# Wider low-half pieces on GpSimd, two reorderings in the first MLP and a later place for two modulation chunks, in a two-layer diffusion block on one core

## The reference

```
ml = split(silu(c) @ w_mod[i] + b_mod[i], 6)       # shift, scale, gate for the mixer, the same for the MLP
h  = rms_norm(xl, g) * (1 + ml[1]) + ml[0]
xl = xl + ml[2] * mixer_i(h)                        # layer 0: Fourier + neighbourhood attention, layer 1: differential attention
h  = rms_norm(xl, g') * (1 + ml[4]) + ml[3]
xl = xl + ml[5] * (square(relu(h @ w_mlp_in[i])) @ w_mlp_out[i])
# context tokens the same way in layer 0 with c_ctx; in layer 1 only the latent tokens go on
return rms_norm(xl, final_norm_g)
```

## Time and profile before

| what | value |
|---|---|
| median of 3 runs | 1603.57 us (1601.69 to 1603.67) |
| the profiled execution | 1603.09 us |
| its span in the trace | 1601.3 us |
| TensorE busy | 1573.3 us, 98% |
| GpSimd busy | 910.0 us, 57% |
| VectorE busy | 894.1 us, 56% |
| ScalarE busy | 604.7 us, 38% |
| low halves of units (L744), 776 pieces of 256 columns | 639.4 us, 856 ns each |
| sums of raw blocks into w_sum (L770), 52 pieces | 48.6 us, 965 ns each |

### The profile page before, as it was taken

How to read it: one execution, slowest core, us unless ns; L and a number is a source line. 1 busy time by engine, 2 the same in 40 slices (tenths; PEclk the granted TensorE clock), 3 DMA queues, 4 the chain that set the end, 5 groups by cost and what they waited for, 6 DMA issues and landing times.

```text
span 1601.3 us, 24059 instructions
## 1 busy us (share of the span) xinstructions
PE 1573.3 (98%) x9272; PEld 1408.7 (88%) x9272; DVE 894.1 (56%) x1364; ACT 604.7 (38%) x1009; POOL 910.0 (57%) x1103
## 2 busy tenths in 40 slices
PE   8999999999899999999999999999999999999998
PEld 5889988988899999999998888878889878888887
DVE  4696457347845656647556746049965753232234
ACT  4422456325252342442542511248853412222222
POOL 2443475326677768768762656354415865555562
PEclk9999999999999999999999999999999999999999
DMA  8574212212042232333352223110003332323221
GB/s 350 197 268 153 93 41 100 80 48 85 27 157 81 80 119 82 116 115 123 105 182 82 91 78 96 66 43 1 1 12 130 129 126 93 105 92 101 83 93 53
DMA packets 50348, 163.15 MB, mean 102 GB/s; under 512 B 6336, under 2 KB 8768, under 8 KB 46656
## 3 DMA queue, kind: packets, MB, share of 16 engines
q1 hardware_dynamic: 50240, 161.68, 29.4%
HBM read 158.78 MB, written 2.10 MB: 100 GB/s over the span
## 4 chain that ended last, share of the span: by engine, by line
PE 86%; DVE 6%; POOL 2%; issue 2%; DMA 2%; ACT 1%; SPq 0%; POOLq 0%; DVEq 0%; ACTq 0%
PE ps L2109 24%; PE ps L2110 24%; PE ps L2111 24%; PE ps L2748 3%; PE ps L2710 2%; PE ps L2737 1%; PE ps L2615 1%; POOL w_lo L744 1%; PE ps L2603 1%; PE ps L2643 1%; PE ps L2427 1%; DVE mod_acc L1439 1%; DMA mod_big<-w_mod_dram 1%; DVE h L1562 1%; DMA raw<-units_dram 1%
## 5 line engine op out<-in xcount | busy, mean ns | idle before, releaser
L744 POOL TENSOR_TENSOR w_lo<-raw,w_hi 128x256 fp32r<-128x256 f32 x776 | 639.4, 856 | 492.4 <-ACT w_hi L949 362.0
L2109 PE MATMUL ps<-h,w_hi 128*128 128x512 f32 (+2 forms) x1016 | 358.0, 352 | 7.2 <-POOL w_lo L744 4.6
L2110 PE MATMUL ps<-h,w_lo 128*128 128x512 f32 (+2 forms) x1016 | 355.3, 350 | 0.0
L2111 PE MATMUL ps<-h,w_hi 128*128 128x512 f32 (+2 forms) x1016 | 355.0, 349 | 0.0
L2109 PEld LDWEIGHTS ps<-h,w_hi 128*128 128x128 f32 x1016 | 192.2, 189 | 32.3 <-issue 9.1
L2111 PEld LDWEIGHTS ps<-h,w_hi 128*128 128x128 f32 x1016 | 192.0, 189 | 17.1
L2110 PEld LDWEIGHTS ps<-h,w_lo 128*128 128x128 f32 x1016 | 192.2, 189 | 16.4
L1660 DVE SCALAR_TENSOR_TENSOR xl<-ps,mods,xl 128x384 f32<-128x384 f32 (+2 forms) x144 | 73.0, 539 | 210.8 <-PE ps L2111 209.0
L949 ACT ACTIVATE w_hi<-raw 128x1024 fp32r<-128x1024 f32 x120 | 126.4, 1054 | 113.2 <-PE ps L2111 107.7
L2109 PE MATMUL ps<-hidl,w_hi 128*128 128x384 f32 (+2 forms) x448 | 150.4, 336 | 2.5 <-DVE hidl L1704 1.5
L2110 PE MATMUL ps<-hidh,w_lo 128*128 128x384 f32 (+2 forms) x448 | 149.8, 334 | 0.0
(11 more groups left out here) (301 smaller groups left out, 3181.1 us busy)
## 6 DMA issues: line engine op xcount, KB each, us to landing
raw<-units_dram SPq DMA_DIRECT2D x187, 512.0 KB, 3.4
mod_ring<-w_mod_dram SPq DMA_DIRECT2D x96, 256.0 KB, 3.9
mod_big<-w_mod_dram SPq DMA_DIRECT2D x16, 1024.0 KB, 10.2
mod_late<-w_mod_dram SPq DMA_DIRECT2D x8, 1024.0 KB, 8.1
xl<-x_dram SPq DMA_DIRECT2D x2, 2048.0 KB, 8.3
bias<-bias_dram SPq DMA_DIRECT2D x8, 384.0 KB, 3.7
xc<-ctx_dram SPq DMA_DIRECT2D x2, 1024.0 KB, 10.4
out_dram<-out_t SPq DMA_DIRECT2D x16, 128.0 KB, 1.8
```

Source lines behind the costliest of these rows:

```text
L744: ins = nc.gpsimd.tensor_tensor(w_lo[:, s, sl], src[:, sl], w_hi[:, s, sl].bitcast(F32), op=ALU.subtract)
L2109: mm(out, a[0], b[1], start=start, stop=False, skip_group_check=onto)
L2110: mm(out, a[1], b[0], start=False, stop=False, skip_group_check=onto)
L2111: return mm(out, a[0], b[0], start=False, stop=stop, skip_group_check=onto)
```

## The change

It has three parts.

1. In the first MLP, ScalarE rounds T4 no longer directly after T3 but after the three weight roundings of `next_block(1)`; on VectorE T1's low half and T2's second sum (`join`) change places.
2. Chunks 10 and 11 are made later in the second MLP's first block: of chunk 10 one step after each of hidden tiles 3 to 6 and four, with the split, after tile 7; of chunk 11 two, three and three steps after the additions behind units 8, 9 and 10. TensorE takes the two sums after units 8 and 11, not after 7 and 10, and VectorE extracts each right before the first addition that needs it. The loads of their rows move as well (MOD_LATE).
3. `lows()` and `mlp()` on GpSimd cut units into two pieces of 512 columns. The first three units, `norm()` and the first MLP keep four pieces of 256.

The diff, cut to its core:

```
-MOD_LATE = {6: (10, (4, 5)), 7: (10, (6, 7)), 8: (11, (0, 1)), 9: (11, (2, 3)), 11: (11, range(4, 8))}
+MOD_LATE = {7: (10, (4, 5)), 9: (10, (6, 7)), 10: (11, range(4)), 12: (11, range(4, 8))}
...
             def lows(first, last, split=0):
                 for u in range(first + AHEAD, last + AHEAD):
-                    low(u, 4)
+                    low(u, 2)
...
                 with pool.Fori(0, HID_BLOCKS - 1) as b:
                     for i in range(16):
-                        low(u0 + i, 4, b)
+                        low(u0 + i, 2, b)
                 for i in range(15 - AHEAD):
-                    low(u0 + 48 + i, 4)
+                    low(u0 + 48 + i, 2)
...
                 turn_high(2, t3h[:], t3f[:])
-                turn_high(3, t4h[:], t4f[:])
...
                 next_block(1)
+                turn_high(3, t4h[:], t4f[:])
...
                 less(t2f[:], t1f[:], 1, 1, H1)
+                turn_low(0, h_lo[:, 0:4, H1], t1f[:], h_hi[:, 0:4, H1])
+                add_tile(0, 2)
                 join(t2f[:], half_f(1, 1, H1))
-                add_tile(0, 2)
-                turn_low(0, h_lo[:, 0:4, H1], t1f[:], h_hi[:, 0:4, H1])
                 add_tile(0, 3)
...
                             if first and i in (8, 12):
+                                extract_late(i // 4 + 8, 6)
                                 dve.wait_ge(mod_done, PE_MODS + i // 4 + 9)
...
                         if first:
-                            if 2 <= i < 6:
-                                mod_step(10, 2 * i - 4)
-                                mod_step(10, 2 * i - 3)
-                            elif i == 7:
-                                extract_late(10, 6)
...
+                            for k in {3: (0,), 4: (1,), 5: (2,), 6: (3,), 7: (4, 5, 6, 7)}.get(i, ()):
+                                mod_step(10, k)
+                            for k in {8: (0, 1), 9: (2, 3, 4), 10: (5, 6, 7)}.get(i, ()):
+                                mod_step(11, k)
...
-                        if first and i in (7, 10):
-                            mod_mm(10 if i == 7 else 11, 6)
+                        if first and i in (8, 11):
+                            mod_mm(10 if i == 8 else 11, 6)
```

## The result

The changed kernel takes **1605.9 us** (median of 20 runs, 1603.88 to 1608.85), the kernel before 1601.66 us (20 runs, 1600.33 to 1603.67). The ratio is **1.0028, 95% interval 1.0022 to 1.0034**: 4.2 us slower. The forecast was 1606.9, with a chance of 0.52 for slower. The profiled execution took 1605.52 us, its span is 1603.7 us.

What follows compares the result with a forecast made beforehand. TensorE, busy 98%, bounds the kernel, so only its waits count: 1603.1 - 4.0 (place A) + 4.1 (late chunks and width) + 2.9 (clock) + 0.8 (elsewhere) = 1606.9 us; range 1601 to 1611.

Steps and rivals of the forecast that it cites:

- The chain's length: First MLP, block 1: GpSimd's seven groups of pieces, started at 410.0, take 31.3 us to p2's low half.
- p2's wait: First MLP, block 1: TensorE no longer waits for p1 but waits 3.9 us for p2's low half.
- The 1.59 us per long step: First MLP: a GpSimd piece meeting a 1536-element VectorE step takes 2.29 us instead of 0.70; six such meetings expected.
- The clock at p2: Behind p2's stall in the first MLP: a fall to 1.2 GHz an even chance, priced 2.9 us; none taken.
- Rival (1): First MLP: the clock falls after p2's stall also, +2.9 us, 1609.8 in all; chance 0.26.
- sign of being wrong: Wrong if both clock falls (p2, chunk 10) or neither are there, chunk 10 waits under 3 us, or p2 doesn't wait.
- my own case: Whole kernel: 1606.9 us, with p2's stall without a clock fall and chunk 10's with one; chance 0.41.
- The three waits: Second MLP, first block: TensorE waits 0.9 us for tile 7, 6.0 for chunk 10, 0.9 for chunk 11.
- The fall behind chunk 10: Second MLP: unit 9 runs at 1.2 GHz behind chunk 10's stall, costing 2.9 us.
- 0.3 us a unit over seven units: Second MLP: 512-column pieces cost VectorE 2.0 us a unit instead of 1.7, 2 us by tile 7.
- two or three units with TensorE close behind: Normalisations around both mixers: wide pieces cost 0.3 us a unit, +0.8 in all, from -0.5 to +1.5.
- The loads: Second MLP: SyncE's row loads for chunk 10 cost nothing; a last row 4 us later would add about 2.

Runs made afterwards that it cites:

- e5: Kernel before plus the two reorderings, with T3's low half and T4's second sum, low half and rounding moved later: 1595.19 us, ratio 0.9958.
- e11: Kernel before with, of the two reorderings, T4's rounding alone: 1601.70 us, ratio 0.9999.
- e12: Kernel before with, of the two reorderings, the move of T1's low half alone: 1601.81 us, ratio 1.0005.
- e1: Kernel before with the two first-MLP reorderings alone: 1600.71 us, ratio 0.9995.
- e6: Changed kernel with 20 further matmuls in front of the wait for chunk 10's sum: 1603.67 us, ratio 1.0010 against the kernel before.
- e3: Kernel before with 512-column pieces alone, in lows() and mlp(): 1611.26 us, ratio 1.0055.
- e7: Kernel before with the second MLP's units in one piece of 1024 columns: 1617.33 us, one run.
- e8: Kernel before with the second MLP's units in eight pieces of 128 columns: 1612.77 us, one run.
- e4: Kernel before with 512-column pieces in the mixers alone (lows()): 1601.48 us, ratio 0.9999.

## Why the prediction held, point by point

**Place A.** The chain's length was worked out as 31.3 us and measured 31.2; p2's wait as 3.9 and measured 3.96; the gain at p2's start as 4.0 and measured 4.0. The 1.59 us per long step is borne out by e5, which took three away and got 5.0. That the stall only moves is shown by e11 and e12: T4's rounding alone brings p2 2.2 us of the 4.0 and T1's low half alone nothing, since the hole grows.

**The clock at p2.** I called it even and took no fall. This step failed: in the traces of the changed kernel, of e1 and of e11 the clock is at its lower level behind p2's stall. Rival (1) was what happened. Its price was 2.9 by the row; the traces gave 1.6 in the changed kernel and 2.85 in e1. I had also named it as a sign of being wrong if both falls are there: both are there. That the time still lies in my own case and not at rival (1)'s 1609.8 is luck, by the sum below.

**Place B.** The three waits were forecast as 0.9, 6.0 and 0.9, and are 1.17, 5.7 and 1.0: 7.8 and 7.9. Alone, at narrow pieces, chunk 10 and 11 were forecast as 4.4 (its own sum, 1288.7 less 1284.4, gives 4.3) and 0.5, and are 5.1 and 0.6. The fall behind chunk 10 was forecast with 2.9; e6 measured 2.2 to 2.9.

**The width.** Its end was right, its way was not. I let VectorE lose 0.3 us a unit over seven units, 2 us by tile 7. In the trace the loss is far larger and shorter: 1.66 us in each tile while GpSimd works without a pause, but that lasts 15.8 us for five units in ten pieces and not 33.9 us for eight units in 32, since a unit takes GpSimd 3.16 us in this company and took 4.23. From tile 4 on GpSimd pauses between units, and VectorE loses 0.8 to 1.0 us to each piece (a step of 0.75 lasts 1.77 at 1267.56), 1.8 to 2.0 us to a unit, near the 2.0 that I had for every unit. The two differences cancel here, and e3 shows that they need not: with two steps of chunk 10 behind each of tiles 2 to 5 the width alone cost 9.8. My working would have put it at 2 us of VectorE's time, 2.9 on top of the late chunks, before the clock. By the Trainium skill ("SBUF — State Buffer", section "SBUF: two separate sides") the lock is held for the whole instruction. For GpSimd's piece e7 and e8 agree with it, at 1024 and at 128 columns, where an even sharing of time would have left the operations at 1.06 us. For VectorE's operation the traces show less: alone it takes 0.43 to 0.69 us (hidden tile 2 in e7), and its turn adds 0.35 on average.

**Elsewhere.** +0.8 was forecast, and e4 shows nothing (1601.48 for 1601.45). The step that failed is "two or three units with TensorE close behind": none that cost time are in the mixers.

**The loads.** Costed at nothing, and nothing shows in the changed kernel: no step of chunk 10 or 11 waits for a row there. In e8 a row is 7.35 us late, beside a second delay.

**The sum.** 1606.9 started from an execution 1.4 us above the median of before, had 0.8 too much elsewhere and 1.6 to 2.9 too little at p2's clock: 1606.9 - 1.4 - 0.8 + 1.6 = 1606.3, for 1605.9 measured. By the traces the change's terms are -4.3 at place A, +1.6 for its clock, +0.3 elsewhere and +6.8 at place B with its clock, 4.4 in all; -4.0, 0, +0.8 and +7.0 were forecast, 3.8 in all. The forecast fell close by wrong terms of either sign; the two stalls were right by themselves.

## What to carry to other kernels

A stall is taken away only where the chain that sets its end gets shorter; here each reordering alone moved most of the idle time into the next link, and both together gained 4 us of which the clock took 1.6 to 2.9 back. Cutting GpSimd's instructions wider made every instruction of VectorE as long as theirs while both were in arrears, so the width is to be judged at the place with a backlog, not by its mean over the program. Before work is put off to a later unit, look for idle time of its engine ahead of the crowd: four steps in a pause of 4.4 us, and three long steps out of a chain on top of the two reorderings, were worth 9 us where the change cost 4.

## What the runs showed of the hardware that I had not expected

How regular the meeting of VectorE and GpSimd is: in the hidden tiles, while both have work waiting, they take turns, and an operation of VectorE lasts the piece's own time and 0.35 us, at each of four widths: 0.78 us beside 128 columns, 1.06 beside 256, 1.61 beside 512, 2.74 beside 1024, where pieces alone take 0.42 (128: sixteen in 6.74 in e8's row), 0.70 (256), 1.27 (512: two in 2.54 in the row below, of the changed kernel) and 2.39 (1024).

```profile
1380.31 2.54 POOL L744 TENSOR_TENSOR w_lo<-raw,w_hi 128x512 fp32r<-128x512 f32 x2 [1.88 <-ACT w_hi L956]
```

How that rule can fail, without a sign beforehand: a VectorE step that comes into a run of pieces can miss its turn and stand until the run is over. Beside the 8.57 us it happened once more in e8's trace (3.30 us at 804.92) and, at the same place of the first MLP, in e12's, both times beside pieces of 256 columns:

```profile
805.48 3.15 DVE L1439 SCALAR_TENSOR_TENSOR mod_acc<-mod_ring,cact,mod_acc 128x512 f32<-128x512 f32 x1 [3.87 <-DMA mod_ring<-w_mod_dram]
...
802.49 5.60 POOL L744 TENSOR_TENSOR w_lo<-raw,w_hi 128x256 fp32r<-128x256 f32 x8
```

The run of eight pieces ends at 808.09, the step at 808.63. The same step took 1.20 us in the trace of before and 1.33 in the changed kernel's, and both executions in which it stood lost 2.1 us there. What decides isn't known.

And that a fall of the clock behind a stall of the same length (3.96 us in the changed kernel and in e1) cost 1.6 us in one execution and 2.85 in another: a mean share of 0.72 and of 0.50 over the 6 us behind it. What decides between them wasn't tried.
